# GLA's gate-up matrix product in split precision, stacked along one contraction of 97 rows, with one weight chunk swept twice

## The reference, cut to what matters

```
q, k, v, g_lr, og = split(h @ w_in)                     # widths 512, 512, 1024, 16, 1024
log_a = log_sigmoid(g_lr @ w_gate_up + gate_bias) / 16  # w_gate_up: 16 x 512
o = gla_chunked(q, k, v, log_a)                         # decays from cumulative sums of log_a
```

## Time and profile before

| what | value |
|---|---|
| median of 3 runs | 1018.91 us (1018.6 to 1020.02) |
| the profiled execution's own time | 1018.6 us |
| its span, first to last instruction | 1016.8 us |
| PE busy | 1010.2 us, 99% |
| PE weight loads busy | 984.5 us, 97% |
| DVE busy | 795.1 us, 78% |
| ACT busy | 646.5 us, 64% |
| POOL busy | 3.0 us |
| granted TensorE clock | full in all 40 slices |

### The profile page before, as it was taken

How to read it: one execution, slowest core, us unless ns; L and a number is a source line. 1 busy time by engine, 2 the same in 40 slices (tenths; PEclk the granted TensorE clock), 3 DMA queues, 4 the chain that set the end, 5 groups by cost and what they waited for, 6 DMA issues and landing times.

```text
span 1016.8 us, 21067 instructions
## 1 busy us (share of the span) xinstructions
PE 1010.2 (99%) x8498; PEld 984.5 (97%) x8498; DVE 795.1 (78%) x952; ACT 646.5 (64%) x890; POOL 3.0 (0%) x9
## 2 busy tenths in 40 slices
PE   9999999999999999999999999999999999999998
PEld 8898999899999999999999999999899999999998
DVE  6879976686666756999887777798996788777787
ACT  7666665565554446677786666676756677656673
POOL 0000000000000000000000000010000000000000
PEclk9999999999999999999999999999999999999999
DMA  9842464355555564634655556454442555555541
GB/s 347 276 178 83 159 224 158 124 180 191 183 203 193 185 243 132 226 131 160 213 202 207 192 195 205 167 192 166 166 166 84 199 216 208 195 192 200 198 149 68
DMA packets 30687, 186.98 MB, mean 184 GB/s; under 512 B 3746, under 2 KB 6659, under 8 KB 8996
## 3 DMA queue, kind: packets, MB, share of 16 engines
q1 hardware_dynamic: 29908, 185.02, 52.0%
q10 hardware_dynamic: 720, 1.11, 0.3%
HBM read 183.99 MB, written 1.34 MB: 182 GB/s over the span
## 4 chain that ended last, share of the span: by engine, by line
PE 99%; DMA 1%; DVE 0%; ACT 0%; SPq 0%; issue 0%
PE g L604 65%; PE d L604 33%; PE d L607 1%; DMA raw<-weights 1%; PE g L607 0%; DVE co_both L1740 0%; DVE w_lo L1740 0%; ACT co_both L1182 0%; ACT w_hi L1182 0%; DVE probs_m_lo L1740 0%; DVE x L1737 0%; DVE ple_mul L1734 0%; SPq L528 0%; SPq L525 0%; ACT ple_sig L1182 0%
## 5 line engine op out<-in xcount | busy, mean ns | idle before, releaser
L1740 DVE TENSOR_TENSOR w_lo<-raw,w_hi 128x2048 fp32r<-128x2048 f32 (+2 forms) x176 | 389.3, 2215 | 91.7 <-ACT w_hi L1182 91.2
L1182 ACT ACTIVATE w_hi<-raw 128x2048 fp32r<-128x2048 f32 (+1 forms) x174 | 326.3, 1878 | 141.6 <-PE g L604 83.6
L604 PE MATMUL g<-f_both,w_hi 128*128 128x256 f32 x1408 | 240.8, 275 | 0.0
L604 PEld LDWEIGHTS g<-f_both,w_hi 128*128 128x128 f32 x1408 | 212.2, 188 | 0.1
L604 PE MATMUL g<-f_both,w_lo 128*128 128x256 f32 x704 | 193.6, 275 | 0.0
L604 PE MATMUL d<-hid_hi,w_hi 128*128 (+1 forms) x528 | 145.2, 275 | 0.0
L604 PE MATMUL d<-hid_lo,w_hi 128*128 (+1 forms) x528 | 145.2, 275 | 0.0
L604 PE MATMUL d<-hid_hi,w_lo 128*128 (+1 forms) x528 | 145.2, 275 | 0.0
L604 PEld LDWEIGHTS g<-f_both,w_lo 128*128 128x128 f32 x704 | 132.1, 188 | 0.0
L604 PE MATMUL g<-x_both,w_hi 128*128 128x256 f32 x704 | 120.0, 275 | 0.0
L604 PEld LDWEIGHTS g<-x_both,w_hi 128*128 128x128 f32 x704 | 106.3, 188 | 0.1
(11 more groups left out here) (371 smaller groups left out, 1947.2 us busy)
## 6 DMA issues: line engine op xcount, KB each, us to landing
raw<-weights SPq DMA_DIRECT2D x168, 1024.0 KB, 4.8
bias_tab<-bias_dram SPq DMA_DIRECT2D x8, 192.0 KB, 7.2
x<-x_t ACTq DMA_DIRECT2D x4, 256.0 KB, 5.4
raw<-weights SPq DMA_DIRECT2D x4, 256.0 KB, 6.5
raw<-weights SPq DMA_DIRECT2D x2, 512.0 KB, 7.6
mem_t<-mem_t SPq DMA_DIRECT2D x1, 1024.0 KB, 9.0
out<-x SPq DMA_DIRECT2D x3, 256.0 KB, 2.2
hy_swap<-hy_qk SPq DMA_DIRECT2D x4, 128.0 KB, 5.9
```

Of the source, the lines that this page charges most:

```text
L604: return pe.matmul(out, lhsT, rhs, start=start, stop=stop, skip_group_check=True)
L1182: return act.activation(out, in_, func, **kw)
L1740: return dve.tensor_tensor(out, a, b, ALU.subtract)
```

## The change

The gate-up is put on split precision. The low-rank stationary operand gets 80 columns: high, low, high, low, high (16 each), so that the 16 low-rank features (times rstd) come out in rows 0 to 79 in that order. The new moving operand `lr_both` (fp32r) has in rows 0 to 31 their rounded values (of the high and the low weights' sums), in rows 32 to 63 what rounding left of the same, in rows 64 to 79 the rounded values once more, and ones in rows 80 to 96. The new stationary operand `gla_up_both` has w_gate_up rounded in rows 0 to 63, its low part in rows 64 to 79, the bias's low part in row 80, zeros in rows 81 to 95, and the rounded bias in row 96. The four matmuls of `gates_up` now have 97 contraction rows and are fp32r. ACT gets one instruction that rounds `gla_up`, DVE one that subtracts (32 rows by 512) ahead of `token_norm`, and the one multiplication into `gla_lr` becomes two multiplications and a subtraction. Chunk 3 is computed by `chunk_in_sweeps`: 32 matmuls with `w_hi`, behind a wait for `hi_done` only, then 16 with `w_lo`, behind `lo_done`. `gla_up` is loaded with 97 rows instead of 33.

```diff
-LR_ROWS = 32
-UP_ROWS = LR_ROWS + 1
+LR_ROWS, LR_LO = 80, slice(32, 64)
+UP_ROWS, UP_LO = 97, slice(64, 96)
...
-        gla_wlr_both = at("gla_wlr_both", TR + 16 * KB + 512, [KT, LR_ROWS], F32R)
-        gla_wlr_hi, gla_wlr_lo = gla_wlr_both[:, :, 0:16], gla_wlr_both[:, :, 16:32]
+        gla_wlr_both = at("gla_wlr_both", TR + 12 * KB + 512, [KT, 3, 2, 16], F32R)
+        gla_wlr_cols = gla_wlr_both[:].rearrange("p k c a r -> p k (c a r)")[:, :, 0:LR_ROWS]
+        lr_both = at("lr_both", H + 51 * KB, [T], F32R)
+        gla_up_both = at("gla_up_both", H + 44 * KB, [512], F32R)
...
+            def chunk_in_sweeps(name, j, moving):
+                c, n = j + FIRST[name], j + FIRST_OUT[name]
+                bank = G[n % U]
...
+                pe.wait_ge(evicted, n - (U - 1))
+                pe.wait_ge(hi_done, c + 1)
+                for k in range(KT):
+                    for f in range(2):
+                        product(k, f, w_hi, 0, start=k == 0 and f == 0)
+                        product(k, f, w_hi, 1)
+                pe.wait_ge(lo_done, c + 1)
+                for k in range(KT):
+                    for f in range(2):
+                        last = product(k, f, w_lo, 0, stop=k == KT - 1)
+                last.then_inc(chunk_done, 1)
...
-                pe.wait_ge(bias_row, 1)
+                pe.wait_ge(up_split, 1)
...
-                        last = mm(D[b][:, f * T:(f + 1) * T], gla_up[0:UP_ROWS, h * P:(h + 1) * P], gla_lr[0:UP_ROWS, :])
+                        last = mm(D[b][:, f * T:(f + 1) * T], gla_up_both[0:UP_ROWS, h * P:(h + 1) * P], lr_both[0:UP_ROWS, :])
...
-            gla_chunk(3)
+            chunk_in_sweeps("gla_in", 3, GLA)
...
-                        fn(gla_wlr_hi, gla_wlr[:]).then_inc(lr_hi_done, 1)
+                        fn(gla_wlr_both[:, :, :, 0, :], wlr_copies(3)).then_inc(lr_hi_done, 1)
...
             gla_ahead(0)
+            fn(gla_up_both[0:UP_ROWS, :], gla_up[0:UP_ROWS, :]).then_inc(up_hi_done, 1)
             rough_rstd()
...
-                    sub(gla_wlr_lo, gla_wlr[:], gla_wlr_hi.bitcast(F32)).then_inc(lr_split, 1)
+                    sub(gla_wlr_both[:, :, 0:2, 1, :], wlr_copies(2), gla_wlr_both[:, :, 0:2, 0, :].bitcast(F32)).then_inc(lr_split, 1)
...
             ahead("gla_in", 0, 0)
+            dve.wait_ge(up_hi_done, 1)
+            sub(gla_up_both[UP_LO, :], gla_up[UP_LO, :], gla_up_both[UP_LO, :].bitcast(F32)).then_inc(up_split, 1)
             token_norm()
             dve.wait_ge(lr_full, count.next(lr_full))
-            mul(gla_lr[0:LR_ROWS, :], D[0][0:LR_ROWS, 0:T], rstd[0:LR_ROWS, :]).then_inc(lr_ready, 1)
+            dve.wait_ge(bias_row, 1)
+            mul(lr_both[0:LR_ROWS, :], D[0][0:LR_ROWS, 0:T], rstd[0:LR_ROWS, :]).then_inc(dve_own, count.one(dve_own))
+            mul(gla_lr[LR_LO, :], D[0][LR_LO, 0:T], rstd[LR_LO, :]).then_inc(dve_own, count.one(dve_own))
+            dve.wait_ge(dve_own, count.sent[dve_own])
+            sub(lr_both[LR_LO, :], gla_lr[LR_LO, :], lr_both[LR_LO, :].bitcast(F32)).then_inc(lr_ready, 1)
             gla_evict(0)
...
-            pool.memset(gla_lr[LR_ROWS:UP_ROWS, :], 1.0).then_inc(bias_row, 1)
+            pool.memset(lr_both[UP_LO.start:UP_ROWS, :].bitcast(F32), 1.0).then_inc(bias_row, 1)
```

More of the change, by code:

```diff
@@ L357, in program, with wlr_copies @@
         o_mean, o_rough, o_newton = row_max[:, 0, :], neg_max[:, 0, :], row_rec[:, 0, :]
-        gla_wlr_both = at("gla_wlr_both", TR + 16 * KB + 512, [KT, LR_ROWS], F32R)
-        gla_wlr_hi, gla_wlr_lo = gla_wlr_both[:, :, 0:16], gla_wlr_both[:, :, 16:32]
+        gla_wlr_both = at("gla_wlr_both", TR + 12 * KB + 512, [KT, 3, 2, 16], F32R)
+        gla_wlr_cols = gla_wlr_both[:].rearrange("p k c a r -> p k (c a r)")[:, :, 0:LR_ROWS]
+        lr_both = at("lr_both", H + 51 * KB, [T], F32R)
+        gla_up_both = at("gla_up_both", H + 44 * KB, [512], F32R)
+        def wlr_copies(n):
+            return gla_wlr[:].unsqueeze(2).broadcast_to([P, KT, n, 16])
         g_banks = stack.enter_context(nc.psum_tensor("g", [P, 4, 512], F32))
@@ L403, in program @@
         hy_half_lo = sem("hy_half_lo")
+        up_hi_done, up_split = sem("up_hi_done"), sem("up_split")
         lr_full, lr_hi_done, lr_split, o_squared = sem("lr_full"), sem("lr_hi_done"), sem("lr_split"), sem("o_squared")
@@ L640, in chunk, with product @@
                         last = mm(to, weights_of(w_lo, c, slot, cols), moving[0][:, k, :], False, k == order[-1])
+                last.then_inc(chunk_done, 1)
+            def chunk_in_sweeps(name, j, moving):
+                c, n = j + FIRST[name], j + FIRST_OUT[name]
+                bank = G[n % U]
+                def product(k, f, part, moved, start=False, stop=False):
+                    cols = slice(k * 2 * P + f * P, k * 2 * P + (f + 1) * P)
+                    return mm(bank[:, f * T:(f + 1) * T], weights_of(part, c, c % U, cols), moving[moved][:, k, :], start, stop)
+                pe.wait_ge(evicted, n - (U - 1))
[8 more added lines that the diff above has]
+                        last = product(k, f, w_lo, 0, stop=k == KT - 1)
                 last.then_inc(chunk_done, 1)
@@ L1070, in low_rank @@
                     for part in range(2):
-                        last = mm(D[0][0:LR_ROWS, 0:T], gla_wlr_both[:, k, :], GLA[part][:, k, :], k == 0 and part == 0, k == KT - 1 and part == 1)
+                        last = mm(D[0][0:LR_ROWS, 0:T], gla_wlr_cols[:, k, :], GLA[part][:, k, :], k == 0 and part == 0, k == KT - 1 and part == 1)
                 return last
@@ L2713, in layout @@
     vectors += [a["ffn_conv_w_2"].reshape(-1, P), a["ffn_conv_b_2"].reshape(-1, P)]
+    bias = a["gla_gate_bias_2"].reshape(1, -1)
     moved = {
@@ L2717, in layout @@
         "p_t": np.stack([features_first(v[0]) for v in a["p_2"]]),
-        "gla_up": np.concatenate([a["gla_w_gate_up_2"][0]] * (LR_ROWS // 16) + [a["gla_gate_bias_2"].reshape(1, -1)]),
+        "gla_up": np.concatenate([a["gla_w_gate_up_2"][0]] * (LR_ROWS // 16) + [bias, np.zeros((15, bias.shape[1]), np.float32), bias]),
         "gla_w_lr": gla_w[:, low_rank:low_rank + 16].reshape(KT, P, 16).transpose(1, 0, 2)}
```

## The result

The changed kernel takes 1020.16 us (median of 22 runs, 1019.5 to 1021.25) against 1018.84 us before (22 runs, 1018.1 to 1020.19). The ratio is 1.0013, with a 95% interval of 1.0007 to 1.0018. So it is 1.3 us slower. I had forecast no change, 1018.9 us, and a range up to 1020.0; the time lies just beyond it.

A forecast was written before the change was run, and what follows sets the result against it. PE was taken as the bound, with DVE equally full around the gate-up. PE's -1.50 us was to be given back as +1.07 + s at chunk 5 and +0.24 at level 2: 1018.9 us, range 1017.3 to 1020.0.

The forecast's parts named there:

- What PE saves: At the gate-up, four fp32r matmuls take 0.46 us instead of 2.00; PE saves 1.54 us, or 1.45 with operand changeover.
- SP's longer `gla_up`: SP's load of gla_up: 128 KB more, landing long before ACT needs it, so no cost was counted.
- the wider low-rank rounding has 0.89: On ACT, the wider rounding of the low-rank weights has 0.89 us of idle time behind it to hide in.
- s: The shift of DVE's chain at rstd and behind it: 0.03 to 0.27 us, taken as 0.2.
- The sum -0.19 + s: Net change: -1.50 at the gate-up, +1.07 + s ahead of chunk 5, +0.24 at level 2; 0.0 with s at 0.2.
- DVE's instructions: DVE's wider low-rank subtraction, new 32-row subtraction and three lr instructions: mean 0.03 to 0.27 us late, lr adding 0.80 to 1.30.
- upper bound: Each new DVE instruction and its follower waits for its forerunner's end: mean at 706.54, 0.27 late; lr instructions add 1.30 us.
- +0.14 of the low-rank subtraction: On DVE, the low-rank subtraction with 256 elements for 128 takes 0.14 us more, moving chunk 2's `w_lo` to 703.50.
- Where the lead goes: PE's gain goes in waits for DVE at chunk 5 (0.43 us of slack) and level 2 (0.19 us of slack).
- DVE comes late: Rival, chance 0.15: DVE's row from rstd to chunk 2's eviction runs over, losing time at level 2; 1019.6 us.
- The lead is kept: Rival, chance 0.20: PE's whole 1.5 us stays past chunk 5 and level 2; 1017.4 us.
- The gate-up doesn't get cheaper: Rival, chance 0.05: fp32r matmuls with 97 rows go at the old distance, no lead for PE; 1018.9 to 1019.0 us.

The follow-up runs named there:

- e2: The kernel before the change with only gla_up loaded as 97 rows, the added 64 being zeros that nothing reads; 1019.57 us, ratio 1.0009.
- e1: The changed kernel with gla_up loaded as 112 rows instead of 97, the added rows being unread zeros; 1018.87 us, ratio 1.0000 to the kernel before.

## Why the prediction was wrong

- **What PE saves: right.** The last matmul ahead of the block starts at 711.01, the first one behind it at 711.67, so the block costs 0.66 - 0.115 = 0.55 us, against 2.00. PE saves 1.45 us, the lower of the two values given. 97 rows and 80 columns cost nothing: the 12 low-rank matmuls took 1.57 us for 1.55.
- **SP's longer `gla_up`: the step that failed.** "SP's longer `gla_up` is 128 KB more, long before ACT needs it." I asked whether `gla_up` itself lands in time, and it does. I didn't ask what the transfer does to the one issued behind it, nor how its shape spreads. The next 1 MB of weights landed after 11.0 us instead of 4.9, 1.82 us too late for ACT, 1.15 us late for DVE's `gla_both`. e2 prices it at 0.8 to 0.9 us in the kernel before, e1 at 1.15 to 1.2 us in the changed one. The difference is mostly a second step that failed with it: "the wider low-rank rounding has 0.89" of idle time holds with the transfer on time (e1 has 0.66 us of it left) and not behind a late one, where its 0.2 us went through. In the prediction's terms all this is a part of s: s was not 0.03 to 0.27 but 1.44 (732.07 - 730.88 = 1.19, and 0.25 us by which this profile was ahead at 670 us), of which 0.27 is DVE's own, as in e1. The sum -0.19 + s then gives +1.25, and +1.32 was measured, +1.21 by the distance. The total comes out, but not place by place: the sum would have PE wait 1.07 + 1.44 = 2.5 us ahead of chunk 5. It lost 1.4 us there (starts at 724.15 and 725.79, a distance of 1.64 for 0.23), as it had already come 1.15 us late to the low-rank product.
- **DVE's instructions: right, at the upper bound.** e1 has the mean at 706.60 (upper bound 706.54) and the lr instructions with the eviction 1.35 us behind the first of them, 1.01 more than the 0.34 before. I had 1.30 for the upper bound, by a slip: 3 x 0.46 less the 0.34 that was there is 1.04. The +0.14 of the low-rank subtraction came as +0.12 (its follower at 697.83 behind 697.50).
- **Where the lead goes: right.** In e1, where the transfer is taken out, PE loses 1.37 us ahead of chunk 5 (starts at 723.34 and 724.94, a distance of 1.60 for 0.23; the sum had 1.07 + s, with s = 0.26: 1.33) and then at level 2, whose first load starts at 731.96, and the end is at +0.02 to +0.17 us against +0.07 from the sum. Had the load had 112 rows, the forecast of 1018.9 would have been met by 1018.87.
- **The rivals.** The outcome is near *DVE comes late* (1019.6 forecast), and its sign came: level 2's first load starts at 732.80, after 732.2, and what s exceeds 0.19 by is lost one to one. But the cause wasn't the one named there; DVE's own new instructions make 0.27 of the 1.44 us of s, and with these alone (e1) the time doesn't change. *The lead is kept* needed two moves that this change hasn't got. *The gate-up doesn't get cheaper* is out. The clock stayed at full through waits of 1.2 us on PE (mean 0.999), so PE lost nothing there.
- **The range** was too narrow above by 0.16 us, as it had no term for a transfer.

## What to carry to other kernels

Ask of every transfer that a change reshapes what it does to those behind it in the queue, and mind its row count: padding 97 rows to 112, a multiple of 16, took back the whole loss, and the 33 rows of the kernel before did no harm. Where idle time is to hide a longer instruction, ask whether it is still there when the engine's input comes late. When two engines are both full in a stretch, a saving on one is worth only the smallest lateness with which it comes to the other's later deliveries; list those (here 0.43 us at chunk 5, 0.19 at level 2, then level 4) before pricing it. Read a PE wait from the distance of matmul starts, since the idle time on the weight loads' row was 0.3 us more than what was lost.

## What the runs showed of the hardware that I had not expected

- A load of 97 rows of 2 KB delayed the 1 MB load issued 5.6 us later: 10.9 and 11.0 us to landing against 4.7 with 112 rows and 4.9 with 33. The load after that landed after 8.4 us in the changed kernel (4.8 before), but nothing waited for it.
- SP's own time for issuing it went the other way, and the next one's too: 0.29 us for 97 rows and then 2.64 for the level masks, against 1.47 and then 0.43 with 112 rows. I can't say why.

```profile
669.37 0.29 SPq L578 DMA_DIRECT2D gla_up<-gla_up  x1
669.71 2.64 SPq L579 DMA_DIRECT2D level_mask_f<-level_mask  x1
```
```profile
669.68 1.47 SPq L578 DMA_DIRECT2D gla_up<-gla_up  x1
671.20 0.43 SPq L579 DMA_DIRECT2D level_mask_f<-level_mask  x1
```
